# A decoder block with memory attention: first scores inside a product, and an output projection of three tiles side by side

## The reference

```python
def stick_breaking_core(q, k, v):       # 16 heads of 64
    z = einsum('bhtd,bhsd->bhts', q, k) * scale
    log_keep = where(earlier, log_sigmoid(-z), 0); csum = cumsum(log_keep)
    w = where(earlier, exp(log_sigmoid(z) + csum[-1:] - csum), 0)
    return einsum('bhts,bhsd->bhtd', w, v)

def mem_cross_attn(h, mem, w_q, w_kv, w_o):     # 4 heads of 256, mem: 256 tokens
    q = _heads(h @ w_q, XA_HEADS)
    k, v = split(mem @ w_kv, 2); k, v = _heads(k), _heads(v)
    p = softmax(einsum('bhtd,bhmd->bhtm', q, k) * (XA_HD ** -0.5))
    return _merge(einsum('bhtm,bhmd->bhtd', p, v)) @ w_o

h = layer_norm(ALPHA * h + stick_breaking(h) @ mix_wo)
h = layer_norm(ALPHA * h + mem_cross_attn(h, mem, w_q, w_kv, w_o))
h = layer_norm(ALPHA * h + conv_ffn(h))          # 1024 -> 2 x 2816 -> 1024
```

## Time and profile before

| | before |
|---|---|
| median of 3 runs | 1365.0 us (1364.82 to 1365.64) |
| the profiled execution's own time | 1364.36 us |
| its span, first to last instruction | 1362.6 us |
| PE busy | 1344.8 us (99%), 9730 matmuls |
| DVE busy | 834.7 us (61%) |
| ACT busy | 702.3 us (52%) |
| POOL busy | 811.6 us (60%) |
| HBM read / written | 119.40 MB / 2.10 MB |

### The profile page before, as it was taken

The page is one execution under the profiler, slowest core; times in us unless marked ns, Lnnn a source line. Parts: engine busy times, 40 slices in busy tenths (PEclk is TensorE's granted clock), DMA queues, the critical chain, the costliest instruction groups (busy, mean ns, idle before and its releaser), DMA issues.

```text
span 1362.6 us, 24461 instructions
## 1 busy us (share of the span) xinstructions
PE 1344.8 (99%) x9730; PEld 1148.5 (84%) x9730; DVE 834.7 (61%) x1073; ACT 702.3 (52%) x1236; POOL 811.6 (60%) x601
## 2 busy tenths in 40 slices
PE   9999999999999999999999999999999999999998
PEld 7888787778899898988888887788888878999987
DVE  5135465466556887885545967344279857777732
ACT  4245566463457566665322478466473525445543
POOL 6643332563366876766655647854268856666782
PEclk9999999999999999999999999999999999999999
DMA  6332221221240223233333212200023222333322
GB/s 228 124 124 77 78 78 47 94 92 62 76 142 32 93 93 109 91 111 105 111 108 109 94 63 93 78 4 4 19 77 124 94 92 94 109 96 106 102 99 77
DMA packets 34517, 122.94 MB, mean 90 GB/s; under 512 B 3824, under 2 KB 4336, under 8 KB 34288
## 3 DMA queue, kind: packets, MB, share of 16 engines
q1 hardware_dynamic: 33696, 119.31, 26.1%
q10 hardware_dynamic: 720, 2.20, 0.5%
HBM read 119.40 MB, written 2.10 MB: 89 GB/s over the span
## 4 chain that ended last, share of the span: by engine, by line
PE 86%; DVE 4%; POOL 3%; issue 3%; ACT 2%; DMA 1%; SPq 0%; ACTq 0%; POOLq 0%; DVEq 0%
PE ps L624 13%; PE ps L626 13%; PE ps L625 13%; PE ps L1515 3%; PE ps L1517 3%; PE ps L1516 3%; POOL w_lo L2390 2%; PE ps L1026 2%; PE ps L1027 2%; PE ps L1028 2%; PE ps L1584 1%; PE ps L1583 1%; PE ps L1585 1%; PE ps L764 1%; PE ps L980 1%
## 5 line engine op out<-in xcount | busy, mean ns | idle before, releaser
L2390 POOL TENSOR_TENSOR w_lo<-stage,w_hi 128x512 fp32r<-128x512 f32 x346 | 511.7, 1503 | 328.0 <-ACT w_hi L1614 321.7
L1614 ACT ACTIVATE w_hi<-stage 128x512 fp32r<-128x512 f32 x312 | 178.9, 623 | 114.1 <-DMA stage<-w 99.0
L624 PE MATMUL ps<-x_hi,w_lo 128*128 128x512 f32 x536 | 213.1, 398 | 0.0
L625 PE MATMUL ps<-x_lo,w_hi 128*128 128x512 f32 x536 | 208.9, 390 | 0.0
L626 PE MATMUL ps<-x_hi,w_hi 128*128 128x512 f32 x536 | 208.8, 390 | 0.0
L624 PEld LDWEIGHTS ps<-x_hi,w_lo 128*128 128x128 f32 x536 | 100.7, 188 | 23.9 <-issue 2.6
L626 PEld LDWEIGHTS ps<-x_hi,w_hi 128*128 128x128 f32 x536 | 100.6, 188 | 21.4
L625 PEld LDWEIGHTS ps<-x_lo,w_hi 128*128 128x128 f32 x536 | 100.7, 188 | 20.8 <-issue 1.0
L2593 POOL TENSOR_TENSOR w_lo<-stage,w_hi 128x512 fp32r<-128x512 f32 x44 | 75.4, 1742 | 54.1 <-DVE s_val L3388 54.1
L2446 POOL TENSOR_TENSOR w_lo<-stage,w_hi 128x512 fp32r<-128x512 f32 x32 | 55.3, 1757 | 34.3 <-DVE us_val L2993 34.3
L2697 DVE TENSOR_TENSOR_SCAN ps<-ps,self_one 128x512 f32<-128x512 f32 (+1 forms) x64 | 49.2, 814 | 26.2 <-ACT ps L1676 26.2
(11 more groups left out here) (558 smaller groups left out, 3839.0 us busy)
## 6 DMA issues: line engine op xcount, KB each, us to landing
stage<-w SPq DMA_DIRECT2D x210, 512.0 KB, 3.5
extra_stage<-w SPq DMA_DIRECT2D x6, 512.0 KB, 5.5
H<-xT SPq DMA_DIRECT2D x3, 512.0 KB, 8.6
mem<-memT SPq DMA_DIRECT2D x2, 512.0 KB, 10.6
pool_n<-pool_count ACTq DMA_DIRECT2D x1, 1024.0 KB, 5.7
outT<-outs SPq DMA_DIRECT2D x4, 256.0 KB, 2.0
outT<-outs SPq DMA_DIRECT2D x2, 384.0 KB, 2.7
stage<-w SPq DMA_DIRECT2D x2, 256.0 KB, 4.1
```

What stands on the lines that cost most here:

```text
L624: pe.matmul(out, wl, hi(k), start=first, stop=False)
L625: pe.matmul(out, wh, lo(k), start=False, stop=False)
L1614: act.activation(unit_hi(b)[:, cols], unit_stage(b)[:, cols], ACT.Copy).then_inc(whi_made, 1)
L2390: pool.tensor_tensor(unit_lo(b)[:, cols], unit_stage(b)[:, cols], unit_hi(b)[:, cols].bitcast(F32), ALU.subtract).then_inc(wlo_made, 1)
```

## The change

In the first attention, `both_scores(0)` is no longer ahead of pair 0's query product but between its blocks 0 and 1. In the second, `xa_scores(0)` stands between blocks 0 and 1 of the third query product, which has bank 6 for that (`XQ_BANKS`) and waits for no evacuation. `mk_hi` has memory of its own, and DVE makes the first head's `mk_hi` and `mk_lo` without waiting for the memory products. The softmax's scale goes into the queries as they are taken (ACT's `take` with a scale, DVE's remainder by a scalar_tensor_tensor), the maximum is negated in its own reduction, and the multiplication of it is gone.

`two_products` waits for the first half of a unit's remainder at the unit's first block, and for the second half at its block 4. In `xo` it takes three tiles, in banks 0, 1 and 2, with 24 blocks in this order: five of tiles 0 and 1 each, then (2,0), the last head's transposes, (0,5), (1,5), the last head's values, (2,1) to (2,5), and blocks 6 and 7 of all three tiles in turn. Tiles 3, 4 and 5 keep banks 1, 0 and 1. ACT rounds unit `xo`+2 ahead of the last head's exponentials and unit `xo`+3 right after the last head's evacuations, ahead of the first square; from there on each unit is rounded one square earlier than before.

```diff
@@ -49,6 +49,7 @@
 EXTRA_PLACES = 4
 XA_KEYS = [1 + 4 * h + 2 * max(h - 1, 0) for h in range(XA_HEADS)]
 XA_VALUES = [2 + 4 * min(h + 2, XA_HEADS) + 2 * h for h in range(XA_HEADS)]
+XA_SCALE = float(D // XA_HEADS) ** -0.5
 LAG = 4
 UP_BANKS = 4
 UP_SEVENTHS = tuple(range(5, 20, 2))
@@ -170,7 +171,7 @@
         mv_hi = at("mv_hi", [P, MEM // P, D], 101.5, F32R)
         mv_lo = at("mv_lo", [P, MEM // P, D], A0 + 40, F32R)
         pT_lo = at("pT_lo", [P, 2, MEM // P, SEQ], A0 + 89, F32R)
-        mk_hi = at("mk_hi", [P, KB, MEM], A0 + 81, F32R)
+        mk_hi = at("mk_hi", [P, KB, MEM], 24, F32R)
         mk_lo = at("mk_lo", [P, KB, MEM], A0 + 32, F32R)
         prob = at("prob", [P, 2, NS, MEM], A0 + 64)
         pT_hi = at("pT_hi", [P, 2, MEM // P, SEQ], A0 + 72, F32R)
@@ -330,6 +331,8 @@
         JOINT_BANK = [(2, 2, 3, 3, 0, 0), (5, 5, 6, 6, 7, 7)]
         DOWN_BANK = [4, 1]
         WO_ACC, WO_ACC2 = 7, 5
+        XQ_BANKS = [0, 1, 6, 1, 0, 1, 0, 1]
+        XO_BANKS = [0, 1, 2, 1, 0, 1]
         WO_BANKS = [1, 0, 3, 6, 4, 0, 1, 3]
         WO_READ = {5: 2, 6: 1, 7: 3}
         XO_BANK = [{6: 0, 7: 1}, {6: 2, 7: 3}]
@@ -648,6 +651,8 @@
                     if ahead is not None and at_n in ahead:
                         ahead[at_n]()
                     if first_n[n] == at_n:
+                        pe.wait_ge(wlo_made, 2 * (u + n) + 1)
+                    if k == KB // 2:
                         pe.wait_ge(wlo_made, 2 * (u + n) + 2)
                     if first_k[k] == at_n:
                         pe.wait_ge(*hi_ready(k))
@@ -781,10 +786,11 @@
             def pair(g):
 
                 u, keys = PAIR_UNIT[g], K_UNITS[g + 1]
-                both_scores(g)
                 if g:
+                    both_scores(g)
                     pe.wait_ge(sb_o, g)
-                product(ps[:, Q_BANK[g + 1], :], u, u % RING, x_rows, x_rows_lo)
+                product(ps[:, Q_BANK[g + 1], :], u, u % RING, x_rows, x_rows_lo,
+                        between=None if g else {1: lambda: both_scores(0)})
                 if g < MK_PAIRS:
                     mem_product(u + 1, 0, 0)
                     turn_shares(g, 0)
@@ -862,9 +868,9 @@
                 elif n == "wo":
                     if t in WO_READ:
                         pe.wait_ge(y_made, WO_READ[t] + BEFORE["y_made"]["wo"] + CREDIT)
-                elif t != 2:
+                else:
                     pe.wait_ge(y_made, t + (BEFORE["y_made"][n] + CREDIT - 1))
-                bank = OUT_BANK(t) if n == "out" else WO_BANKS[t] if n == "wo" else 6 if t == 2 else u % 2
+                bank = OUT_BANK(t) if n == "out" else (WO_BANKS if n == "wo" else XO_BANKS)[t]
                 product(ps[:, bank, :], u, u % RING, hi, lo, between=between)
 
             def o_rows(k):
@@ -927,12 +933,14 @@
                     two_products(U0["xq"], x_rows, x_rows_lo, lambda k: (xhi_made, k + 1 + BEFORE["xhi_made"]["wo"]),
                              lambda k: (x_ready, k + 1 + BEFORE["x_ready"]["wo"]))
                 for d in range(2 if h else 0):
-                    u = U0["xq"] + 2 * h + d
-                    pe.wait_ge(evac, EV0["xq"] + 2 * h + d + CREDIT - 1)
-                    product(ps[:, u % 2, :], u, u % RING, x_rows, x_rows_lo)
+                    n, u = 2 * h + d, U0["xq"] + 2 * h + d
+                    if n > 2:
+                        pe.wait_ge(evac, EV0["xq"] + n + CREDIT - 1)
+                    product(ps[:, XQ_BANKS[n], :], u, u % RING, x_rows, x_rows_lo,
+                            between={1: lambda: xa_scores(0)} if n == 2 else None)
                 if h:
                     xa_turn(h - 1)
-                xa_scores(h)
+                    xa_scores(h)
                 if h:
                     xa_values(h - 1)
             def xo_sums(half, parts=range(2)):
@@ -958,9 +966,11 @@
 
             pe.wait_ge(evac, EV0["xo"] + CREDIT)
             two_products(U0["xo"], o_rows, o_rows_lo, lambda k: (xa_o, k + 1), lambda k: (xa_o, k + 1),
-                         [(n, k) for k in range(KB) for n in range(2)],
-                         {10: lambda: xa_turn(XA_HEADS - 1), 12: lambda: xa_values(XA_HEADS - 1)})
-            for t in range(2, KB - 2):
+                         [(n, k) for k in range(5) for n in range(2)] + [(2, 0), (0, 5), (1, 5)] + [(2, k) for k in range(1, 6)]
+                         + [(n, k) for k in range(6, KB) for n in range(3)],
+                         {10: lambda: pe.wait_ge(xa_exp, NS * XA_HEADS), 11: lambda: xa_turn(XA_HEADS - 1),
+                          13: lambda: xa_values(XA_HEADS - 1)}, banks=XO_BANKS)
+            for t in range(3, KB - 2):
                 tile("xo", t, o_rows, o_rows_lo)
             for t in (6, 7):
                 pe.wait_ge(y_made, t - 1 + (BEFORE["y_made"]["xo"] + CREDIT))
@@ -1744,12 +1754,12 @@
 
 
             def xa_soft(h):
-                act.wait_ge(xa_max, 3 * h + 3)
+                act.wait_ge(xa_max, 2 * h + 2)
                 if h >= 2:
                     act.wait_ge(xa_turned, 2 * (h - 1))
                 for t in range(NS):
                     act.activation(prob[:, h % 2, t, :], ps[:, 2 + t // 2, (t % 2) * MEM:(t % 2 + 1) * MEM], ACT.Exp,
-                                   bias=soft_max[:, h, t:t + 1], scale=float(D // XA_HEADS) ** -0.5,
+                                   bias=soft_max[:, h, t:t + 1],
                                    accum_out=soft_sum[:, h, t:t + 1]).then_inc(xa_exp, 1)
 
             def xa_take(h):
@@ -1768,14 +1778,16 @@
                     u = U0["xq"] + 2 * h + d
                     if h:
                         split_hi(u + 2)
-                    take(xq_hi[:, 2 * h + d, :], u % 2, u + CREDIT + 1)
+                    take(xq_hi[:, 2 * h + d, :], XQ_BANKS[2 * h + d], u + CREDIT + 1, scale=XA_SCALE)
                 if h == 0:
                     split_hi(U0["xq"] + AHEAD)
                 if h:
                     xa_take(h - 1)
+                if h == XA_HEADS - 1:
+                    split_hi(U0["xo"] + 2)
                 xa_soft(h)
-            split_hi(U0["xo"] + 2)
             xa_take(XA_HEADS - 1)
+            split_hi(U0["xo"] + AHEAD)
 
             def xo_square(n):
                 act.wait_ge(y_made, n + (1 + CREDIT + BEFORE["y_made"]["xo"]))
@@ -1802,8 +1814,8 @@
 
             for n in range(7):
                 xo_square(n)
-                if n < 5:
-                    split_hi(U0["xo"] + n + AHEAD)
+                if n < 4:
+                    split_hi(U0["xo"] + n + AHEAD + 1)
                 if n in (4, 5):
                     split_hi(U0["up"] + 2 * (n - 4))
                     split_hi(U0["up"] + 2 * (n - 4) + 1)
@@ -2798,10 +2810,7 @@
                 for b in range(2):
                     dve.tensor_reduce(soft_max[:, h, 2 * b:2 * b + 2],
                                       ps[:, 2 + b, :].rearrange("p (t n) -> p t n", t=2), mybir.AxisListType.X,
-                                      ALU.max).then_inc(xa_max, 1)
-                dve.wait_ge(xa_max, 3 * h + 2)
-                dve.tensor_scalar(soft_max[:, h, :], soft_max[:, h, :], -float(D // XA_HEADS) ** -0.5, None,
-                                  ALU.mult).then_inc(xa_max, 1)
+                                      ALU.max, negate=True).then_inc(xa_max, 1)
                 dve.wait_ge(xa_exp, NS * (h + 1))
                 link(dve.reciprocal(soft_sum[:, h, :], soft_sum[:, h, :]))
                 dve.tensor_tensor(prob[:, h % 2, :, :], prob[:, h % 2, :, :],
@@ -2823,14 +2832,14 @@
             def xa_parts(h):
 
                 two = slice(2 * h, 2 * h + 2)
-                if h == 0:
-                    dve.wait_ge(evac, EV0["xq"] + CREDIT)
+                if h in (0, XA_HEADS - 1):
+                    dve.wait_ge(evac, EV0["xq" if h else "mem"] + CREDIT)
                 link(dve.tensor_copy(mk_hi[:, two, :], mem_k[:, two, :]))
                 dve.tensor_tensor(mk_lo[:, two, :], mem_k[:, two, :], mk_hi[:, two, :].bitcast(F32), ALU.subtract).then_inc(xa_split, 1)
                 for d in range(2):
                     dve.wait_ge(evac, EV0["xq"] + CREDIT + 2 * h + d + 1)
-                    dve.tensor_tensor(xq_lo[:, 2 * h + d, :], ps[:, d, :], xq_hi[:, 2 * h + d, :].bitcast(F32),
-                                      ALU.subtract).then_inc(xa_split, 1)
+                    dve.scalar_tensor_tensor(out=xq_lo[:, 2 * h + d, :], in0=ps[:, XQ_BANKS[2 * h + d], :], scalar=XA_SCALE,
+                                             in1=xq_hi[:, 2 * h + d, :].bitcast(F32), op0=ALU.mult, op1=ALU.subtract).then_inc(xa_split, 1)
                 two = slice(2 * h * P, (2 * h + 2) * P)
                 link(dve.tensor_copy(mv_hi[:, :, two], mem_v[:, :, two]))
                 dve.tensor_tensor(mv_lo[:, :, two], mem_v[:, :, two], mv_hi[:, :, two].bitcast(F32), ALU.subtract).then_inc(xa_split, 1)
@@ -2848,7 +2857,7 @@
                 cols = xo_cols(n)
                 if half is None:
```

(2 more changed lines are left out.)

## The result

The changed kernel takes 1367.34 us (median of 22 executions, the lowest 1365.51), the kernel before 1364.99 (22 executions beside them, 1364.04 to 1366.41). The ratio is 1.0013, with a 95% interval of 1.0007 to 1.0019: 0.13% slower, inside the 0.2% that count as no change, and inside the range. Four executions that took 1.7 times as long or more (4707.55 us here, 6446.21 in e4, 2826.62 and 2358.06 of the kernel before) are left out of all that follows. But the predicted 1366.4 lies where no execution is. The 21 that are left form two groups: 8 between 1365.51 and 1366.29, with a mean of 1365.8, and 13 between 1367.06 and 1368.27, with a mean of 1367.7. The profiled execution is one of the upper group: 1367.84 us, span 1366.1 us.

A forecast was written before the change was run, and what follows sets the result against it. PE was taken to bound the kernel, busy for 1344.8 of 1362.6 us. The terms 0.0 - 0.38 + 0.0 + 1.83 gave +1.45 us, a median going from 1365.0 to 1366.4 us, with a range of 1364.2 to 1368.0.

The forecast's parts named there:

- First attention, 0.0 us: First attention's scores: the block fills the wait for `k_hi`, but PE then waits for DVE's shares at the transposes; 0.0 us.
- Second attention, -0.38 us: Second attention's first scores: the block gains 0.68 us, POOL slowed by the early `mk_hi` and `mk_lo` gives back 0.30.
- The five matmuls' slip of 0.1 us: Second attention: the five held-back matmuls slip by about 0.1 us, because the last `x_lo` comes later.
- The rule of the Trainium skill: Second attention: POOL blocks for both DVE instructions, `x_lo` slips 1.11 us and the edit loses 0.1; not used in the sum.
- Half waits, 0: `two_products`: only the second query unit's `w_lo` is late, and next blocks wait for ACT's `x_hi` anyway; 0 us.
- `xo`, the first tiles, -0.73 us: `xo` before tile 3: the waits at the transposes (0.52 us) and at (0,6) (0.21) both go; 0.73 us earlier.
- `xo`, tile 3, a wait of 2.46 us: `xo`: tile 3 waits 2.46 us for bank 1, behind DVE's `xo_y(1)`; net for `xo` +1.83 us.
- Tile 4, 1.7 us to spare: `xo`: after tile 0's end, rounding and the first half of `w_lo` leave tile 4 1.7 us to spare.
- rival (c): After tile 3's stall PE's clock falls; one product at the lower level costs 5.44 us more, 1371.8 us; chance 0.06.
- the last of its own signs: After the wait at tile 3 in `xo`: the prediction is wrong if the clock reads below 1.00.

The follow-up runs named there:

- e4: The changed kernel with two further useless DVE copies ahead of `xo_y(1)`, lengthening the gap at tile 3; 1368.34 us, ratio to the kernel before 1.0020.
- e6: e1 with the first attention's first scores ahead of the query product again, as before the change; 1363.72 us, ratio to the kernel before 0.9987.
- e7: e1 without the scans of two of four query blocks for pair 0's second head, so less DVE work; one execution, 1364.2 us.
- e5: e1 with DVE's first `mk_hi` and `mk_lo` held back until the memory products are taken; 1363.25 us, ratio to the kernel before 0.9988.
- e1: The changed kernel with tile 3 of `xo` in PSUM bank 3, waiting for no evacuation; 1363.79 us, ratio to the kernel before 0.9992.
- e3: The changed kernel with only tiles 0 and 1 of `xo` side by side again, as before; 1364.14 us, ratio to the kernel before 0.9994.
- e2: The changed kernel with DVE's `xo_y(1)` moved ahead of the sums of tile 0; 1364.51 us, ratio to the kernel before 0.9997.
- e8: e5 with pair 0's second turned shares ahead of key product block 4 instead of 3; 1363.09 us, ratio to the kernel before 0.9982.

## Why the prediction was right, and where it was not

**First attention, 0.0 us: right.** 18.39 us for 18.37, a wait of 0.54 us at the transposes for the 0.65 that was foretold. e6 and e7 show from both sides that it is the same wait moved down the stream.

**Second attention, -0.38 us: right.** It was -0.34. The stretch of POOL's `x_lo` was taken as 0.62 us and is 0.63, and e5 shows the 0.30 us that it gives back. The first `w_lo` of the unit was the mechanism: the block starts with it. The five matmuls' slip of 0.1 us was underestimated, it is 0.27 (1.56 for 1.29), but it ends ahead of that `w_lo` and costs nothing of its own. The rule of the Trainium skill ("SBUF — State Buffer", "Who interferes with whom"), read in the prediction as POOL blocking for the whole of both DVE instructions, asked for 1.11 us. The traces show 0.61 to 0.63 (10.70 against 10.07 and 10.09), so the measurement goes against that figure here. The section also says that whichever engine issues first has the ports and the other waits, and in that the traces agree with it, as the last section shows: DVE's pair lost 1.60 us (1.04 + 1.67 for 0.42 + 0.69), POOL 0.63.

**Half waits, 0: right.** In the stage's beginning PE waited 0.40 us for `w_lo` at the second unit's first block before (286.26 for 285.86), and no longer does. But from the stage's first matmul to the one behind the last wait for `x_hi` it is 6.17 us both times (285.32 to 291.49, 285.70 to 291.87): the other waits took its place.

**`xo`, the first tiles, -0.73 us: right in kind.** Both waits are gone. The stretch from the first block to the end of the five matmuls is 19.93 us, where 20.14 was foretold: with each wait went its slow restart as well, 0.11 us at (0,6) and 0.06 at the transposes, which the term left out.

**`xo`, tile 3, a wait of 2.46 us: right.** It is 2.46 in the trace, at the place, for the instruction and as the longest of PE's waits in the kernel. Net for `xo` up to tile 3: +1.52, and +1.63 with tile 3's restart, for +1.83.

**Tile 4, 1.7 us to spare: right in kind**, with a slip in the sum: from tile 0's end at 373.43 to tile 3's start at 376.57 the prediction's own times make 3.14 us and not 2.7. POOL has the first half of tile 4's `w_lo` at 377.97 + 1.27 = 379.24 us, and without the fall of the clock the tile would start at 376.38 + 5.44 + 0.11 = 381.93: 2.7 us to spare. Without the stall there is none left: in e1 and e5 tile 4's `w_lo` is 0.17 us late.

**The clock: wrong.** By the terms above the median would be 1364.99 + 0.0 - 0.34 + 1.63 = 1366.3, and the group of 8 executions that by this account kept their clock lies 0.5 us below it, at 1365.8. The other 13 lie 1.9 us higher. The step that failed is rival (c), dismissed with "a single gap of 2.5 us between dense stretches I hold to be too little", a sentence with no row behind it, as the prediction itself said that no row shows what a longer wait does. Its size was off in the other direction. It was priced at a whole product at the lower level, 5.4 us. The fall lasted 3.4 us and cost 1.66. Even a whole product would cost less: 24 x (0.427 - 0.227) = 4.8 us by the pitch of the slow rows. And the earlier trace rows, from which the two levels were read, do not show them by themselves, since the granted clock reads 1.00 there (1.6 to 5.0 us); the slow rows of the changed kernel, at 0.50, do. So the mechanism was named and both its chance (0.06 for 13 of 21) and its price were mis-sized. By the last of its own signs, a clock below 1.00 after the wait, the prediction is wrong here. That the median still fell inside the range was luck: the range leaves this rival out, and its upper end stands for other terms. A better working would have taken the fall as a coin with a bounded price: nothing, or some part of a product.

That the gap is what takes the clock down is shown by the executions of one chip. No gap at tile 3 (e1, e3): 0 of 24 in an upper group. 1.09 us (e2): 0 of 12. 3.39 us (e4): 8 of 11. The changed kernel, with 2.46 us, adds 13 of 21. e5, e6 and e8, without the gap, add 33 executions, none above 1365.13. That each of the upper executions fell at this place is inferred; it was seen there in the two that were profiled. The clock's mean over the whole span fits, though it is weak evidence: in the changed kernel it reads 1.000 in 7 of the 8 lower executions and 0.998 or 0.999 in 12 of the 13 upper ones (3.7 us at 0.54 are 0.001 of the span), in e4 1.000 in the 3 lower and 0.997 to 0.999 in the 8 upper. But 10 executions of the kernel before with ordinary times (1364.2 to 1365.9) read 0.999 as well, so that mean by itself marks no fall. Nor is the kernel before free of slow executions: 4 of 82 were at 1367.1 to 1369.1 with a mean of 0.998 or 0.999, and where the clock fell in those is not known.

## What to carry to other kernels

When tiles run side by side end together, count the banks for the tile after them: the one that is taken next must not be one whose evacuation is second in another engine's list, or PE waits for the whole list. Price a new PE gap by its length, and where it is as long as the one here, add the clock: a fall in more than half of the executions at 1.7 to 2.1 us each, which nearly doubles what the 2.46 us cost. A block put into a wait ahead of a chain moves the wait to the end of that chain unless the chain starts sooner, so look there first; one block more in front of the chain's consumer (e8) took all but 0.1 us of it away where the earlier start (the change) could not.

## What the runs showed of the hardware

PE's granted clock after a gap between dense stretches was left to chance from one execution to the next: 1.09 us never, 2.46 us in 13 of 21 executions, 3.39 us in 8 of 11. In the changed kernel's profiled execution it did not fall during the gap or at the restart but 1.2 us behind it, for 3.4 us of dense work at the level of 1.2 GHz (0.50 from 377.7 to 380.7). In e4's it fell inside the gap, 2.2 us after PE had stopped, and stayed down for 6.8 us. So a gap can bring the fall while PE stands or only after it works again. What decides between two executions of the same program was not found, and no kernel here separates the length of the gap from where it lies. The Trainium skill ("TensorE: Matmul & The Clock Gate", "What's actually happening") has the clock follow how busy PE has recently been, with which this agrees in direction.

A DVE cast and a two-input remainder (0.42 and 0.69 us alone) that overlap POOL's `x_lo` took 1.04 and 1.67 us, and cost POOL 0.6 us. The single rows show how. The cast starts at 292.11 in the middle of an `x_lo` and ends at 293.15, 0.32 us after the next one starts at 292.83; the remainder ends at 294.86, 0.59 us after the one at 294.27. The two distances are 0.32 to 0.33 and 0.58 to 0.59 us in the kernel before, e1 and e5 too (against `w_lo` in the first and the last), whenever DVE starts: in the kernel before the cast takes 1.46 us and still ends 0.32 after POOL's next start. POOL's two instructions take 1.44 and 1.70 us from start to start for 1.25. So DVE seems to wait for the end of the POOL instruction that runs, and POOL's next one is then held up, by 0.19 and 0.45 us, less than DVE's instruction takes alone. That such a wait is what the rows show is inferred from their ends.
